# Two attention layers hand over to their output projections: columns turned in the last block, weights split ahead

## The reference, cut to what matters

```python
def diff_attention(...):            # layer 0: 8 heads of width 128
    ...
    a = p[:, :, 0] - lam * p[:, :, 1]
    o = einsum('bhqk,bkhe->bqhe', a, v)          # "weighing"
    o = o * rsqrt(mean(o * o) + LN_EPS)          # per head
    o = o * subln_g * (1 - lam_init)
    return o.reshape(B, S, H * dv) @ w_out       # output projection

def moba_attention(...):            # layer 1: 16 heads of width 64, one block of 256 keys
    ...
    return o @ w_out

h = layer_norm(ALPHA * h + mix, ...)
h = layer_norm(ALPHA * h + square(relu(h @ w_up)) @ w_down, ...)
```

## Time and profile before

| | |
|---|---|
| runs shown | 1491.90, 1492.46, 1492.96 us |
| profiled execution, its span | 1491.44 us, 1489.6 us |
| TensorE busy | 1320.5 us, 89% of the span |
| VectorE, ScalarE, GpSimd busy | 953.6, 553.3, 379.3 us |
| end of attention in layer 0 | about 107 to 125 us of the span |
| its output projection | 125.0 to 148.7 us |
| end of attention in layer 1 | about 434.6 to 447.4 us |
| its output projection | 447.4 to 470 us |
| expert layer (DMA at about 421 GB/s) | from about 820 us to the end |

### The profile page before, as it was taken

How to read it: one execution, slowest core, us unless ns; L and a number is a source line. 1 busy time by engine, 2 the same in 40 slices (tenths; PEclk the granted TensorE clock), 3 DMA queues, 4 the chain that set the end, 5 groups by cost and what they waited for, 6 DMA issues and landing times.

```text
span 1489.6 us, 19343 instructions
## 1 busy us (share of the span) xinstructions
PE 1320.5 (89%) x6330; PEld 939.4 (63%) x6330; DVE 953.6 (64%) x2272; ACT 553.3 (37%) x1153; POOL 379.3 (25%) x383
## 2 busy tenths in 40 slices
PE   7998899998988999999799788789798978888888
PEld 5986799997986999987588544334353534344333
DVE  4575655565555555575785677676767677676765
ACT  3553544454554444455573222222222122122221
POOL 0103000000001000000552544544434344345440
PEclk9997999999999999999899899999999999999999
DMA  9714565654304755553600999999999999999997
GB/s 353 256 57 101 170 190 177 197 194 195 120 29 123 229 185 192 174 206 105 205 29 1 389 420 421 421 421 421 421 422 421 422 421 421 422 421 421 421 421 310
DMA packets 97245, 406.82 MB, mean 273 GB/s; under 512 B 6923, under 2 KB 44364, under 8 KB 60332
## 3 DMA queue, kind: packets, MB, share of 16 engines
q0 software_dynamic: 39552, 276.60, 45.5%
q1 hardware_dynamic: 57644, 129.60, 25.3%
HBM read 404.84 MB, written 1.07 MB: 272 GB/s over the span
## 4 chain that ended last, share of the span: by engine, by line
PE 44%; DMA 23%; DVE 14%; issue 13%; POOL 3%; ACT 2%; DVEq 0%; SPq 0%; POOLq 0%; ACTq 0%
DMA ring<-in_peer_uv,prob 21%; PE ps L655 12%; PE ps L656 12%; PE ps L657 12%; PE ps L787 4%; DMA uv_gain<-in_peer_uv,prob 2%; DVE w_low L1800 1%; POOL small L1581 1%; DMA ring<-in_v_a 1%; DVE prob L2338 1%; DVE prob L2326 1%; DVE ring L2462 1%; DVE arena_u L2462 1%; PE ps L606 1%; DVE prob L2374 0%
## 5 line engine op out<-in xcount | busy, mean ns | idle before, releaser
L1800 DVE TENSOR_TENSOR w_low<-ring,w_high 128x1024 fp32r<-128x1024 f32 x140 | 165.1, 1222 | 174.3 <-ACT w_high L1159 174.0
L1159 ACT ACTIVATE w_high<-ring 128x1024 fp32r<-128x1024 f32 x142 | 142.3, 1052 | 204.1 <-PE ps L657 204.1
L655 PE MATMUL ps<-hT_high,w_high 128*128 128x256 f32 x512 | 145.1, 283 | 0.3
L656 PE MATMUL ps<-hT_low,w_high 128*128 128x256 f32 x512 | 144.7, 283 | 0.0
L657 PE MATMUL ps<-hT_high,w_low 128*128 128x256 f32 x512 | 144.7, 283 | 0.0
L1403 ACT ACTIVATE prob<-prob 128x4 f32<-128x4 f32 (+2 forms) x67 | 13.8, 206 | 347.2 <-DVE prob L2462 347.2
L1391 ACT ACTIVATE sco<-const,prob 128x128 f32<-128x128 f32 x256 | 84.2, 392 | 151.5 <-DVE prob L2472 138.6
L787 PE MATMUL ps<-arena_v,sco 128*128 128x512 f32 x256 | 121.4, 619 | 19.2 <-ACT sco L1391 19.2
L1587 POOL TENSOR_SCALAR small<-small 128x1 f32<-128x1 f32 x8 | 2.4, 305 | 524.9 <-ACT arena_v L1197 524.9
L787 PE MATMUL ps<-ring,sco 128*128 128x512 f32 x192 | 102.1, 682 | 32.3 <-ACT sco L1391 32.3
L787 PE MATMUL ps<-arena_u,sco 128*128 128x512 f32 x256 | 115.6, 600 | 8.2 <-ACT sco L1391 8.2
(11 more groups left out here) (444 smaller groups left out, 3072.9 us busy)
## 6 DMA issues: line engine op xcount, KB each, us to landing
ring<-in_w_up SPq DMA_DIRECT2D x32, 1024.0 KB, 5.5
ring<-in_w_down SPq DMA_DIRECT2D x32, 1024.0 KB, 4.8
qkring<-in_qk_a SPq DMA_DIRECT2D x8, 1024.0 KB, 4.9
qkring<-in_qk_b SPq DMA_DIRECT2D x8, 1024.0 KB, 4.8
ring<-in_peer_wq SPq DMA_DIRECT2D x8, 1024.0 KB, 9.0
ring<-in_w_in SPq DMA_DIRECT2D x8, 860.0 KB, 5.2
ring<-in_v_a SPq DMA_DIRECT2D x4, 1024.0 KB, 13.0
ring<-in_w_out_a SPq DMA_DIRECT2D x4, 1024.0 KB, 13.9
```

The lines of the kernel that those rows point to most:

```text
L655: pe.matmul(dst, a[0], b[0], start=start, stop=False, skip_group_check=True)
L656: pe.matmul(dst, a[0], b[1], start=False, stop=False, skip_group_check=True)
L1159: sc.activation(w_split[pair][0][:, part], ring[:, slot, part], ACT.Copy)\
L1800: ve.tensor_tensor(w_split[pair][1][:, part], ring[:, slot, part], w_split[pair][0][:, part].bitcast(F32), ALU.subtract)\
```

## The change

It does four things, the same in both layers.

1. `turn_pair(j, bank)` turns one pair of column blocks (four transposes). Pairs 0 and 1 are turned in block 7 between its scores and `turn_probs`; pair 2 behind the last weighing; pair 3 between the second and the third group of products. `nat_ready` now is signalled once after `finish(5)` and once after `finish(7)`.
2. Two further places for split chunks are laid over buffers of the attention: `w_split[2]` over the split values, `w_split[3]` over the splits of q and k. Chunks 0 to 3 go to places 1, 3, 2, 1, and the first chunk of `w_up` to place 2.
3. Chunk 0 is split inside block 6 (ScalarE, VectorE), chunk 1 inside block 7, chunk 2 behind it. The low part of the turned columns goes to `hT_low_qkv`, since place 1 and the buffers over it are now in use earlier.
4. The third and fourth `hT_split` waits of `split_natural` thereby stand ahead of pairs that are turned late.

```diff
+            def turn_pair(j, bank):
+                for cc in range(2):
+                    for t in range(NT):
+                        last = pe.transpose(ps[bank][:, cc * S + t * P:cc * S + t * P + P],
+                                            nat[:, t, (2 * j + cc) * P:(2 * j + cc + 1) * P], ident)
+                last.then_inc(sem("turned_s"), 1)
...
                 if more:
                     project(1 - b, 0, reverse=True)
+                else:
+                    pe.wait_ge(sem("nat_ready"), count.take("nat_ready"))
+                    turn_pair(0, 4)
+                    turn_pair(1, 5)
                 turn_probs(b)
...
             def split_natural():
+                pe.wait_ge(sem("hT_split"), count.take("hT_split"))
+                turn_pair(2, 4)
                 for j in range(4):
                     slot = (turn[0] + j) % 4
-                    pe.wait_ge(sem("hT_split"), count.take("hT_split"))
+                    if j:
+                        pe.wait_ge(sem("hT_split"), count.take("hT_split"))
+                    if j == 2:
+                        pe.wait_ge(sem("nat_ready"), count.take("nat_ready"))
+                        turn_pair(3, 6)
...
-                    if j < 3:
-                        last.then_inc(sem(f"w{j % 2}_used"), 1)
+                    if j % 2 == 0:
+                        last.then_inc(sem(("w1_used", "", "w0_used")[j]), 1)
...
             attention_layer(P, first=True)
-            turn_over(nat, ready="nat_ready", split=True)
             split_natural()
...
-                attend_block(0, split=False)
-                attend_block(1, more=False, split=False)
+                exps(0)
+                take_projection(1, 0)
+                sc.wait_ge(sem("qk_split1"), count.take("qk_split1", 8))
+                split_high(0, 1, halves=(0,))
+                take_probT()
+                split_high(0, 1, halves=(1,))
+                take_projection(1, 1)
+                exps(1)
+                take_turned_high(reverse=True, pairs=(0, 1))
+                split_high(1, 3, halves=(0,))
+                take_probT()
+                split_high(1, 3, halves=(1,))
...
             def out_and_mlp():
-                split_high(0, 0)
-                split_high(1, 1)
-                take_turned_high(reverse=True)
-                split_high(2, 0, "w0_used")
+                take_turned_high(reverse=True, pairs=(2,))
+                split_high(2, 2)
+                take_turned_high(reverse=True, pairs=(3,))
                 split_high(3, 1, "w1_used")
-                split_high(0, 0, "w0_used")
+                split_high(0, 2, "w0_used")
...
                 for f in range(8):
                     attend_block(f, f % 2, finish, first=(f == 0), split=(f < 6))
+                    if f == 6:
+                        ve.sem_inc(sem("nat_ready"), 1)
+                        split_low(0, 1)
+                take_turned_low(hT_low_qkv, reverse=True, pairs=(0, 1))
+                split_low(1, 3)
                 finish(7, 1)
...
-                split_low(0, 0)
-                split_low(1, 1)
-                take_turned_low(reverse=True)
-                split_low(2, 0)
+                take_turned_low(hT_low_qkv, reverse=True, pairs=(2,))
+                split_low(2, 2)
+                take_turned_low(hT_low_qkv, reverse=True, pairs=(3,))
                 split_low(3, 1)
-                split_low(0, 0)
+                split_low(0, 2)
```

More of the change, by code:

```diff
@@ L200, in build @@
             qk_split = [[split(f"{name}_{part}", [P, D]) for part in ("high", "low")] for name in "qk"]
+        with ExitStack() as over:
+            split("pad_to_w2", [P, 2048], F32)
+            w_split.append([split("w2_high", [P, 2048]), split("w2_low", [P, 2048])])
+            split("pad_to_act", [P, 15472 - 6144], F32)
+            w_split.append([split("w3_high", [P, 2048]), split("w3_low", [P, 2048])])
         with ExitStack() as over:
@@ L647, in take_half @@
             def take_half(pair, half, slot):
-                pe.wait_ge(sem(f"w{pair}_split"), count.take(f"w{pair}_split"))
+                pe.wait_ge(sem(f"w{pair % 2 if pair < 2 else 0}_split"), count.take(f"w{pair % 2 if pair < 2 else 0}_split"))
                 if half:
@@ L740, in mlp @@
             def mlp():
-                up(0, first=True, pair=0)
+                up(0, first=True, pair=2)
                 up(1)
@@ L1139, in take_tile, with take_turned_high @@
                         .then_inc(sem("hT_a"), 1)
-            def take_turned_high(reverse=False):
-                for c in range(4):
+            def take_turned_high(reverse=False, pairs=range(4)):
+                for c in pairs:
                     sc.wait_ge(sem("turned_s"), count.take("turned_s"))
-                    dst, src = hT_high[:, 2 * c:2 * c + 2, :], ps[4 + c][:, :]
+                    dst, src = hT_high[:, 2 * c:2 * c + 2, :], ps[(4, 5, 4, 6)[c] if reverse else 4 + c][:, :]
                     if reverse:
@@ L1150, in take_turned_high, with split_high @@
                     sc.activation(dst, src, ACT.Copy).then_inc(sem("hT_high"), 1)
-            def split_high(slot, pair, free=None, width=2048):
-                sc.wait_ge(sem(f"raw{slot}_landed"), count.take(f"raw{slot}_landed", 16))
+            def split_high(slot, pair, free=None, width=2048, halves=range(2)):
+                if 0 in halves:
+                    sc.wait_ge(sem(f"raw{slot}_landed"), count.take(f"raw{slot}_landed", 16))
                 if free:
                     sc.wait_ge(sem(free), count.take(free))
-                for half in range(2):
+                for half in halves:
                     part = slice(half * D, min((half + 1) * D, width))
@@ L1781, in take_rows, with take_turned_low @@
                                  ALU.mult).then_inc(sem("hT_v"), 1)
-            def take_turned_low(low=hT_low, reverse=False):
-                for c in range(4):
+            def take_turned_low(low=hT_low, reverse=False, pairs=range(4)):
+                for c in pairs:
                     ve.wait_ge(sem("hT_high"), count.take("hT_high"))
                     part = slice(2 * c, 2 * c + 2)
-                    dst, src, high = low[:, part, :], ps[4 + c][:, :], hT_high[:, part, :].bitcast(F32)
+                    bank = (4, 5, 4, 6)[c] if reverse else 4 + c
+                    dst, src, high = low[:, part, :], ps[bank][:, :], hT_high[:, part, :].bitcast(F32)
                     if reverse:
```

15 lines of the change are left out of this document (8 added, 7 removed).

## The result

| | before | changed |
|---|---|---|
| median, 5 runs each | 1491.90 us | 1476.97 us |
| lowest and highest | 1489.73, 1492.96 | 1474.48, 1482.42 |
| profiled execution, its span | 1491.44, 1489.6 | 1476.59, 1474.8 |

The ratio of the runs is 0.9893, 95% interval 0.9872 to 0.9914: the change makes the kernel about 1.1% faster, 12.8 to 19.1 us. The forecast was 1480.1 with a range of 1475.5 to 1485.0. So direction and range held. The medians lie 14.9 us apart where the sum was 12.4, and the trace shows by which of the cases.

A forecast was written before the change was run, and what follows sets the result against it. TensorE, busy 89% of the span, was taken as the bound, waiting before the first product of each layer's projection. Gains of 8.9 and 3.5 us, 12.4 off 1491.44, give 1479.0; the median lies 1.0 above: 1480.1, range 1475.5 to 1485.0.

The forecast's parts named there:

- the sum: Predicted gain over both layers: 8.9 us in layer 0 plus 3.5 in layer 1, 12.4 us off the profiled 1491.44.
- What bounds: Between last weighing and first product TensorE waits on four `w_low` of VectorE (4.63 us) in each layer; behind, nothing waits.
- The work that left the chain: First product 8.6 us earlier in layer 0, 4.9 in layer 1, less 0.46 each for pair 3's transposes between products.
- The splits in the earlier blocks and the eight early transposes at nothing: Block 6's added copies and subtractions cost nothing; block 7's eight transposes take 0.9 us inside a 1.51 us TensorE pause.
- ScalarE's three instructions ahead of the probabilities: Block 7: 2.0 us more on ScalarE; nothing lost in layer 0, second half of layer 1's weighing 0.6 us late.
- The supply: Layer 0 copies and splits keep pace with the products; block 7's finish begins at 117.3, chunk 3 ready about 132.5.
- The rival of a failing supply: TensorE waits some 2 to 3 us between product groups in each layer; 1485 to 1487 us, chance 0.08.
- the slower one: Late columns hold block 7 as a whole in both layers; above 1495 us, chance 0.03.
- The clock: Falls in block 7, rises at 117.8 and 444.5; low-clock products lose 0.65 us in layer 0, 0.9 in layer 1.
- The second rival: Clock does not fall at all in block 7; gains 11.2 and 5.4 us, total 16.6, 1476 us, chance 0.15.
- The rest: Everything behind the projections runs as before, with 2.5 us to either side for starts behind a pause.
- The weighed rule: Skill's claim that transposes don't engage full clock; by it the gain is 9.4 us, 1483.1; the forecast kept the middle.

The follow-up runs named there:

- splits alone: Changed kernel with the weight splits early but all 16 transposes in one piece behind `finish(7)`; 1492.79 us, ratio to before 0.9999.
- turns alone: Changed kernel with early turning kept, splits of chunks 0 and 1 put back behind the last block; 1487.25 us, ratio to before 0.9959.
- kernel before kept warm: Kernel before with identity transposes that nothing reads in all pauses of both handovers; 1492.79 against 1492.80 us, ratio 0.9987.
- late pairs: Changed kernel with pairs 0 and 1 turned behind the last weighing, ScalarE's copy of the probabilities moved ahead; 1483.67 us, ratio to before 0.9929.
- probabilities first: Changed kernel with ScalarE's first half of chunk 1's split moved behind the copy of the turned probabilities; 1475.34 us, ratio to before 0.9886.
- second set: The changed kernel run once more, unchanged, on the same chip as the kernel before with warm pauses; 1479.61 us, ratio to before 0.9895.
- filler alone: Kernel before with eight identity transposes that nothing reads in block 7 between scores and turned probabilities; 1492.32 against 1491.98 us, ratio 0.9997.
- filler behind the projection: Changed kernel with 44 transposes that nothing reads behind the projection's products, in the layer norm's pause; 1477.82 us, ratio to before 0.9895.

## Why the prediction held, and where it was off

**What bounds.** Right. The splits and the turn stood between the last weighing and the first product, and nothing but TensorE stood behind. But the views named the `w_low` as the chain's link, and the experiments show that this link alone is worth little: splits alone shorten the two handovers by 2.6 us, a part of it by the clock, turns alone by 5.1, together they give 16.6. The chain of waits shows the one path that ended last; the second lay 1.3 us beside it (14.06 for 15.40 in layer 0). The prediction had both in its sum, as one step, and so did not need to tell them apart.

**The work that left the chain.** Right, and this is most of the gain: 8.6 - 0.46 = 8.1 and 4.9 - 0.46 = 4.4 us in the sum, 8.4 and 4.6 by the difference to the kernel before kept warm.

**The splits in the earlier blocks and the eight early transposes at nothing.** Right. From the scores of block 6 to those of block 7 it is 8.74 us in both kernels, and the transposes take 1.09 us in a pause of 1.51. As the late pairs show, their being early is worth 3.3 us in layer 0 and, against the kernel with the probabilities first, 4.7 in layer 1, the clock's part included.

**ScalarE's three instructions ahead of the probabilities.** Right: nothing in layer 0, and in layer 1 a wait, forecast 0.6 us, measured 0.82. It is larger because the first half of the weighing ended sooner at full clock (counted from the turned probabilities, 0.4 us sooner than in the sum, and the copy only 0.25). It cost 0.9 us, as its removal shows.

**The supply.** Right: the finish of block 7 began at 117.5 (forecast 117.3), chunk 3 was split at 130.9 (forecast 132.5), and TensorE was busy for 22.81 of 22.85 us. The rival of a failing supply has nothing for it, nor has the slower one.

**The clock.** This is the term that was off. The sum took a fall in block 7 as before and 0.65 and 0.9 us lost behind it; in the profiles of the changed kernel there was none. So 11.0 and 5.6 us came for 8.9 and 3.5. The second rival gives 11.2 and 5.4 and is what happened in the handovers; it had 0.15. It was priced right and believed too little. Its first product comes at 115.18 and not at 114.8: 0.3 is the later start, and with the clock up the last thing ahead of pair 2 is no longer the weighing (ended at 114.5) but VectorE's first `hT_low` (114.7). For the mechanism that the rival named, work of TensorE in block 7's pause, there is this count in layer 0. Without transposes there (before, splits alone, late pairs) the clock falls ahead of the weighing, at 111.0, 111.8 and 112.7, in three profiles of three. With eight or more of them it is full to the end of the weighing in eight profiles of nine; the ninth is the turns alone, which fell at 112.9 with the same transposes in the same pause. So they make the difference in most executions and do not ensure it; what decides in the ninth is open.

**The rest.** The forecast said that everything behind runs as before, with 2.5 us to either side for the starts behind a pause. That is too narrow: the hybrid attention alone took 169.0 to 175.8 us in twelve profiles, and no edit touches it. The scatter was underrated from the start, on three runs that lay within 0.1% of each other: later runs of the kernel before go from 1489.77 to 1500.72. Between the two profiles of the changed kernel it differs by 5.9 us, and the spans by 3.2 only because in the second one block 7 began 1.3 sooner and the expert layer was 1.1 shorter. That layer, forecast as long as before, took 1.3 us more in the first profile and 0.2 in the second. The range of 1475.5 to 1485.0 held the median, but one of the changed kernel's first five runs lies below it. That the medians come so near to 1480.1 (1476.97, and 1479.61 in the second set) is in part luck: the handovers gave 16.6 us and not 12.4, and what lies behind them took a part of the surplus back.

**The weighed rule.** The sum by the rule that transposes do not bring the full clock was 9.4 us. More runs bear on it: with 44 transposes as TensorE's only work from the last product to 143 the clock stayed at 1.00, where it had fallen at 142.5 without them, and the warm kernel before stayed there through 30 of them. And in the filler alone it rose at 121.4, when TensorE had done only transposes since 118.48. So in these traces fp32 transposes hold the full clock and bring it, against what the Trainium skill ("TensorE: Matmul & The Clock Gate", Part 4: PE-mode transpose) states.

## What to carry to other kernels

When an in-order engine holds several preparations between a last and a first product, count the paths that end there together: here removing the one that the chain of waits shows gave no time that the runs can tell, and removing both shortened the two handovers by 16.6 us, 3.6 of them clock. Work whose inputs are ready a block earlier belongs into the pauses of the last block, on each of the engines that it passes. And when a kernel that holds a full clock in one stretch gains there and not in total, look at the next pause: compare a stretch with itself over several profiles before you believe a difference of a few microseconds.

## What the runs showed of the hardware that was not expected

Full clock won in one stretch did not by itself shorten the kernel. In the filler alone, in the filler behind the projection and in the warm kernel before, full clock was won over several microseconds and the medians did not move (ratios to before 0.9997 and 0.9987; for the filler behind, 1477.8 against 1477.0 and 1479.6 of the changed kernel). For the two fillers the traces show a later fall that took the gain back (445.7, 337.4); for the warm kernel no trace shows where it went. A low clock can also last long under steady work: some 17 us, 728 to 745, with TensorE busy for 16.21 of 17.00 us. It had begun in a stretch with pauses (one of 1.72 us ended at 726.99), and the same stretch of the first profile ran at full clock. Why it did not rise sooner is not shown.
